# Hybrid streaming encoder step on one core: last SSM group written out with y's split moved ahead of its exponents, bias tables loaded between the slabs

## The reference, cut to what matters

```
h = rmsnorm(x, norm_mix[0])
proj = h @ attn_w_in                       # qi, ki, k, v, q
score = sum_h relu(qi . ki) * wi * IDX_SCALE;  top_k of the visible keys
logits = q . k_sel * ATTN_SCALE + rel_bias[rel_bucket(position difference)]
x = x + softmax(logits) @ v_sel @ attn_w_o;    x = x + mlp(x)
...
z, xBC, dt = rmsnorm(x, norm_mix[1]) @ ssm_w_in;  xBC = silu(conv4(xBC))
# per group g of 8 (4 heads of 64, state 128):
y = (C B^T * decay) (x dt) + C prev_state exp(a_cs) + x * d_skip
y = group_rmsnorm(y * silu(z)) * ssm_norm
x = x + y @ ssm_w_out;    x = x + mlp(x);    out = rmsnorm(x, norm_final)
```

## Time and profile before

| | |
|---|---|
| median of 3 runs | 1992.48 us (1989.91 to 1995.55) |
| the profiled execution | 1994.71 us, its span 1992.7 us |
| mean granted TensorE clock | 0.974 |
| busy: TensorE, VectorE, ScalarE, GpSimd | 1892.0, 1277.9, 796.2, 300.1 us |
| DMA | 176.81 MB, 89 GB/s over the span |

### The profile page before, as it was taken

How to read it: one execution, slowest core, us unless ns; L and a number is a source line. 1 busy time by engine, 2 the same in 40 slices (tenths; PEclk the granted TensorE clock), 3 DMA queues, 4 the chain that set the end, 5 groups by cost and what they waited for, 6 DMA issues and landing times.

```text
span 1992.7 us, 35226 instructions
## 1 busy us (share of the span) xinstructions
PE 1892.0 (95%) x13063; PEld 1769.6 (89%) x13063; DVE 1277.9 (64%) x2367; ACT 796.2 (40%) x1417; POOL 300.1 (15%) x353
## 2 busy tenths in 40 slices
PE   7899888799999999999999999999799999999998
PEld 7777455599999999999889888988699999999998
DVE  4378674435858676546777777777653685858654
ACT  4222473234434343333555345553533443434332
POOL 0001551020000000021333332324102000000001
PEclk9999799999999999998999999999899999999999
DMA  7632102322232223223233443334333222232321
GB/s 163 114 67 51 54 2 92 88 71 79 70 89 77 85 70 102 74 66 90 80 115 124 124 135 89 116 112 127 130 106 105 71 73 80 81 89 69 92 75 53
DMA packets 311565, 176.81 MB, mean 89 GB/s; under 512 B 39888, under 2 KB 305040, under 8 KB 310416
## 3 DMA queue, kind: packets, MB, share of 16 engines
q1 hardware_dynamic: 308752, 172.49, 30.6%
q10 hardware_dynamic: 2688, 2.62, 0.4%
HBM read 155.18 MB, written 19.72 MB: 88 GB/s over the span
## 4 chain that ended last, share of the span: by engine, by line
PE 66%; DVE 5%; ACT 4%; issue 4%; DVEq 0%; ACTq 0%
PE psum L1326 26%; PE psum L204 20%; PE psum L1354 13%; DVE prev L711 2%; PE psum L583 1%; DVE conv_out L700 1%; ACT WH L194 1%; PE psum L587 1%; PE psum L570 1%; PE psum L536 1%; ACT L975 1%; ACT Wm L923 1%; ACT HH L1435 0%; PE psum L611 0%; ACT prevT L883 0%
## 5 line engine op out<-in xcount | busy, mean ns | idle before, releaser
L204 PE MATMUL psum<-b2H,WH 128*128 128x320 f32 x912 | 218.9, 321 | 13.1 <-DVE b2L L1137 12.2
L204 PE MATMUL psum<-b2H,WL 128*128 128x320 f32 x912 | 209.5, 311 | 0.0
L204 PE MATMUL psum<-b2L,WH 128*128 128x320 f32 x912 | 209.4, 311 | 0.0
L194 ACT ACTIVATE WH<-W 128x1024 fp32r<-128x1024 f32 x90 | 95.0, 1056 | 232.8 <-PE psum L204 206.9
L1326 PE MATMUL psum<-b2H,HT 128*128 128x320 f32 x816 | 186.3, 310 | 1.1 <-DVE xT L423 1.1
L1326 PE MATMUL psum<-b2L,HT 128*128 128x320 f32 x816 | 186.0, 309 | 0.0
L204 PEld LDWEIGHTS psum<-b2H,WH 128*128 128x128 f32 x912 | 151.0, 191 | 27.7 <-issue 26.5
L198 DVE TENSOR_TENSOR WL<-W,WH 128x1024 fp32r<-128x1024 f32 x90 | 134.4, 1494 | 55.1 <-ACT WH L194 54.7
L1354 PE MATMUL psum<-HH,HT 128*128 128x320 f32 x544 | 167.4, 308 | 1.5 <-DVE HL L1443 1.5
L1354 PE MATMUL psum<-HL,HT 128*128 128x320 f32 x544 | 167.8, 308 | 0.0
L204 PEld LDWEIGHTS psum<-b2L,WH 128*128 128x128 f32 x912 | 154.3, 190 | 0.0
(11 more groups left out here) (393 smaller groups left out, 4436.1 us busy)
## 6 DMA issues: line engine op xcount, KB each, us to landing
W<-ssm_w_in SPq DMA_DIRECT2D x98, 256.0 KB, 3.1
RW<-mlp_w_up SPq DMA_DIRECT2D x64, 256.0 KB, 3.0
RWx<-mlp_w_up SPq DMA_DIRECT2D x64, 256.0 KB, 3.1
RW<-mlp_w_down SPq DMA_DIRECT2D x64, 256.0 KB, 3.1
RWx<-mlp_w_down SPq DMA_DIRECT2D x64, 256.0 KB, 3.2
bc<-scratch_acs SPq DMA_DIRECT2D x8, 1280.0 KB, 7.6
W<-attn_w_in SPq DMA_DIRECT2D x32, 256.0 KB, 3.7
prev<-state_ssm SPq DMA_DIRECT2D x16, 512.0 KB, 5.2
```

The lines of the kernel that those rows point to most:

```text
L194: act.activation(WH[:, b.slot], W[:, b.slot], ACT.Copy).then_inc(w_hi, 1)
L204: last = pe.matmul(psum[0:m, 2 * b.slot + h, 0:TH], w[:, b.slot, k, 0:m], r[:, k, h * TH:(h + 1) * TH], start=(n == 0 and i == 0), stop=(n ...
```

## The change

Two places. At the start the bias product goes to banks 2 and 3 and the turned vectors to bank 0. TensorE begins slab 0's chunks once the vectors are copied, and slab 1's chunks come one step later in the interleaving and wait for the bias copy. ScalarE makes the high parts of x chunks 2 and 3 ahead of slab 1's split, and VectorE does x's low parts 2 and 3 and the copy of chunk 4 ahead of its part of slab 1's split. SP issues four biasP loads, slab 5, four biasP loads, slab 6, the biasS loads and then slabs 7 and 8.

In the SSM, ScalarE's and VectorE's loops run over groups 2 to 6, and group 7 is written out with `last=True`. There ScalarE makes y's high parts 0 to 7 between the two halves of group 7's exponents. VectorE does the first two states of group 7, the scaling of group 6's y and y's low parts 0 to 3, then its `split_lo` of block B_OUT+1, then low parts 4 to 7 and the last two states. TensorE's, GpSimd's and SP's lists keep their order there.

```diff
     def prompt_states(dve, g):
-        n = 13 * g
+        first_states(dve, g)
+        later_states(dve, g, 1, 4)
+
+    def first_states(dve, g):
         dve.wait_ge(tCS, g + 1)
...
         dve.tensor_copy(ST[:, 0], cs[:, 0:256]).then_inc(sts, 1)
-        for t in range(1, 4):
+
+    def later_states(dve, g, t0, t1):
+        n, cs = 13 * g, bank(4, 1024, 2)
+        for t in range(t0, t1):
...
@@ ssm_group_dve
-        z_evac(dve, g, 1, (lambda: y_scaled(dve, u)) if L else None)
-        prompt_states(dve, g)
+        if last:
+            ssm_last_dve(dve, g, u)
+        else:
+            z_evac(dve, g, 1, (lambda: y_scaled(dve, u)) if L else None)
+            prompt_states(dve, g)
+
+    def ssm_last_dve(dve, g, u):
+        def then():
+            first_states(dve, g)
+            later_states(dve, g, 1, 2)
+            y_scaled(dve, u)
+            for k in range(4):
+                y_split_dve(dve, k)
+        z_evac(dve, g, 1, then)
+        for k in range(4, 8):
+            y_split_dve(dve, k)
+        later_states(dve, g, 2, 4)
@@ ssm_group_act
-        exponents(act, g, lambda: split_hi(act, b0(5), 4))
+        def halfway():
+            split_hi(act, b0(5), 4)
+            if last:
+                for k in range(8):
+                    y_split_act(act, k)
+        exponents(act, g, halfway)
@@ tail_act (tail_dve alike)
-        with act.Fori(2, SG) as g:
+        with act.Fori(2, SG - 1) as g:
             ssm_group_act(act, g, g - 1)
+        ssm_group_act(act, SG - 1, SG - 2, True)
         u = SG - 1
-        for k in range(8):
-            y_split_act(act, k)
@@ SP
-            for p0 in range(0, P, DS):
-                sp.dma_start(biasP[p0:p0 + DS], ...)
+            for p0 in range(0, 64, DS):
+                load_bias_p(p0)
+            load_slab(sp, Block(5), slab_g1(5))
+            for p0 in range(64, P, DS):
+                load_bias_p(p0)
+            load_slab(sp, Block(6), slab_g1(6))
             for gj in range(8):
                 sp.dma_start(biasS[DS * gj:DS * gj + DS], ...)
...
-            for b in range(5, 9):
-                load_slab(sp, Block(b), slab_g1(b))
+            load_slab(sp, Block(7), slab_g1(7))
+            load_slab(sp, Block(8), slab_g1(8))
@@ TensorE
-            pe.matmul(psum[0:NH, 0, 0:512], rb_stage[:], oh_stage[:, 0:512], start=True, stop=True)
-            pe.matmul(psum[0:NH, 1, 0:NREL - 512], ...)
+            pe.matmul(psum[0:NH, 2, 0:512], rb_stage[:], oh_stage[:, 0:512], start=True, stop=True)
+            pe.matmul(psum[0:NH, 3, 0:NREL - 512], ...)
-                pe.transpose(psum[:, 2, col:col + rows], ...).then_inc(v_turn, 1)
-            pe.wait_ge(v_rdy, 5)
+                pe.transpose(psum[:, 0, col:col + rows], ...).then_inc(v_turn, 1)
+            pe.wait_ge(v_rdy, 4)
             first_products(0, 0)
             turn_x(4)
             first_products(0, 1)
-            first_products(1, 0)
             turn_x(5)
             first_products(0, 2)
-            first_products(1, 1)
+            pe.wait_ge(v_rdy, 5)
+            first_products(1, 0)
...
@@ ScalarE
             x_hi(1)
+            x_hi(2)
+            x_hi(3)
             split_hi(act, Block(1))
-            x_hi(2)
             act.wait_ge(v_turn, 2)
+            act.wait_ge(v_rdy, 4)
...
@@ VectorE
-            split_lo(dve, Block(1))
-            chunk_lo(dve, 2, 2, 0, b1H, b1L)
-            for d in range(4, KC):
+            chunk_lo(dve, 2, 2, 0, b1H, b1L)
+            take_x(4)
+            chunk_lo(dve, 3, 3, 0, b1H, b1L)
+            split_lo(dve, Block(1))
+            for d in range(5, KC):
```

More of the change, by code:

```diff
@@ L792, in y_scaled, with ssm_group_dve @@
                                      ALU.mult, ALU.mult).then_inc(yo, 1)
-    def ssm_group_dve(dve, g, u):
+    def ssm_group_dve(dve, g, u, last=False):
         L = u is not None
@@ L929, in exp_w, with ssm_group_act @@
         act.activation(Wm[:], Wm[:], ACT.Exp, scale=-1.0).then_inc(ee, 1)
-    def ssm_group_act(act, g, u):
+    def ssm_group_act(act, g, u, last=False):
         L = u is not None
@@ L2017, in tail_dve @@
         ssm_group_dve(dve, 1, 0)
-        with dve.Fori(2, SG) as g:
+        with dve.Fori(2, SG - 1) as g:
             ssm_group_dve(dve, g, g - 1)
+        ssm_group_dve(dve, SG - 1, SG - 2, True)
         u = SG - 1
-        for k in range(8):
-            y_split_dve(dve, k)
         add_to_x(dve, Block(B_OUT), 0)
@@ L2088, in _, with load_bias_p @@
             bt = S["bias"]
-            for p0 in range(0, P, DS):
+            def load_bias_p(p0):
                 sp.dma_start(biasP[p0:p0 + DS], skew(bt, -REL0 - P - p0, [[NREL - 1, DS], [DS * NREL, NH], [1, 256]])
                              ).then_inc(bias_in, 16)
+            for p0 in range(0, 64, DS):
[4 more added lines that the diff above has]
+            load_slab(sp, Block(6), slab_g1(6))
             for gj in range(8):
@@ L2252, in _ @@
             pe.wait_ge(c_in, 112)
-            pe.matmul(psum[0:NH, 0, 0:512], rb_stage[:], oh_stage[:, 0:512], start=True, stop=True)
-            pe.matmul(psum[0:NH, 1, 0:NREL - 512], rb_stage[:], oh_stage[:, 512:NREL],
+            pe.matmul(psum[0:NH, 2, 0:512], rb_stage[:], oh_stage[:, 0:512], start=True, stop=True)
+            pe.matmul(psum[0:NH, 3, 0:NREL - 512], rb_stage[:], oh_stage[:, 512:NREL],
                       start=True, stop=True).then_inc(v_turn, 1)
             for n, (rows, col) in enumerate(((56, 0), (P, 64), (32, 192))):
-                pe.transpose(psum[:, 2, col:col + rows], v_stage[0:rows, n], ident[0:rows, 0:rows]).then_inc(v_turn, 1)
-            pe.wait_ge(v_rdy, 5)
+                pe.transpose(psum[:, 0, col:col + rows], v_stage[0:rows, n], ident[0:rows, 0:rows]).then_inc(v_turn, 1)
+            pe.wait_ge(v_rdy, 4)
             first_products(0, 0)
@@ L2261, in _ @@
             first_products(0, 1)
-            first_products(1, 0)
             turn_x(5)
             first_products(0, 2)
-            first_products(1, 1)
+            pe.wait_ge(v_rdy, 5)
+            first_products(1, 0)
             turn_x(6)
             first_products(0, 3)
-            first_products(1, 2)
+            first_products(1, 1)
             turn_x(7)
             first_products(0, 4)
+            first_products(1, 2)
             first_products(1, 3)
@@ L2533, in _ @@
             x_hi(1)
+            x_hi(2)
+            x_hi(3)
             split_hi(act, Block(1))
-            x_hi(2)
             act.wait_ge(v_turn, 2)
-            act.activation(tb_stage[:], psum[0:NH, 0:2, :].rearrange("p a b -> p (a b)")[:, 0:NREL], ACT.Copy).then_inc(v_rdy, 1)
+            act.wait_ge(v_rdy, 4)
+            act.activation(tb_stage[:], psum[0:NH, 2:4, :].rearrange("p a b -> p (a b)")[:, 0:NREL], ACT.Copy).then_inc(v_rdy, 1)
             for t in range(NT):
-                if t < 4:
-                    x_hi(t + 3)
+                if t < 3:
+                    x_hi(t + 4)
                 x_squares(t)
@@ L2682, in _ @@
             for dst, n0, w in ((vcol[:, 16:56], 16, 40), (cw[:].rearrange("p t r -> p (t r)"), 64, P), (cb_[:], 192, 32)):
-                dve.tensor_copy(dst, psum[:, 2, n0:n0 + w]).then_inc(v_rdy, 1)
+                dve.tensor_copy(dst, psum[:, 0, n0:n0 + w]).then_inc(v_rdy, 1)
+            chunk_lo(dve, 2, 2, 0, b1H, b1L)
+            take_x(4)
+            chunk_lo(dve, 3, 3, 0, b1H, b1L)
             split_lo(dve, Block(1))
-            chunk_lo(dve, 2, 2, 0, b1H, b1L)
-            for d in range(4, KC):
+            for d in range(5, KC):
                 take_x(d)
```

## The result

The changed kernel takes 1970.87 us (median of four, 1970.02 to 1977.16), the kernel before, run beside it, 1992.18. The ratio is 0.9898 [0.9873, 0.9924], 20.3 us less (25.3 to 15.1). Forecast: 1972, 20.6 us less. Timed a second time beside other experiments, it gave 0.9898 [0.9877, 0.9918] and a median of 1970.67 us. One of those six executions was a slow one of 9095 us; it isn't in the ratio, and the median without it is 1970.20. The profiled execution is the slowest of its four (1977.16 us, span 1975.4, mean granted clock 0.976), so I read it for places and durations, and the profile of the second timing (span 1968.4, clock 0.980) for lengths of stages.

A forecast was written before the change was run, and what follows sets the result against it. TensorE, busy 95% of the span, was taken to bound the kernel through its stands and low clock. Start 8.9 us plus handover 11.7 makes 20.6 off 1992.48: forecast 1972, range 1966 to 1981.

The forecast's parts named there:

- First product: Kernel start: TensorE begins at 15.35, 2.5 us earlier, of which 1.6 us is kept at slab 2's products (bounds 0 and 2.5).
- Bias loads: SP's queue between slabs: the 5.16 us stand ahead of slab 5 goes, and 2.1 us of slow clock with it.
- the covers: Slack between a slab's split and TensorE's demand behind the bias loads: 4.7 us for slab 5, 2.4 for slab 6.
- Rival (b): Bias part yields only 1.6 us: slab 5 not ahead, or slab 6 takes the stand over; 1979 us, chance 0.10.
- two halves of 0.9: Slab 5's load behind four biasP loads: each half takes 0.9 us, an estimate, so it lands at 49.8.
- The later stages have no time of their own: After the start each stage waits on the one before, so the start's 8.9 us gain passes through whole.
- Handover: Last SSM group to output projection: stand 2.8 us for 12.2, gain 11.4 us, less 0.3 for a new wait.
- the new wait of 0.3 for the sample states: Second output block: VectorE's states end at 1424.3, TensorE asks at 1424.1; 0.3 us wait, bounds 0 and 2.
- Written-out group: Last SSM group outside the loop on VectorE and ScalarE: shorter stand there, gain 0.6 us, bounds 0 and 1.0.
- (a): The handover gives 3 to 8 us back, through the clock and waits without cover; 1975 to 1980 us, chance 0.19.
- (c): The handover yields nothing because y's loads are what really ends the wait; 1983.5 us, chance 0.06.
- (d): Slower: engines wait for the new code of the last group written out; 1998 us and up, chance 0.03.

The follow-up runs named there:

- six_ahead: The changed kernel with six biasP loads, not four, ahead of slab 5 on SP; 1973.13 us, ratio 0.9919 to the kernel before.
- eight_ahead: The changed kernel with all eight biasP loads ahead of slabs 5 and 6, biasS still behind; 1973.97 us, ratio 0.9923 to the kernel before.
- start_only: The kernel before with only the start changed (banks, first products, order of loads on SP), SSM as before; 1984.0 us, ratio 0.9972.
- product_held: The kernel before with GpSimd's product of weights in the last group held until y's eight low parts are done; 1988.28 us, ratio 0.9985.
- states_first_both: The changed kernel with both halves of VectorE's sample states ahead of the slab splits in each SSM group; 1943.68 us, ratio 0.9752 to the kernel before.
- written_out_only: The kernel before with ScalarE's and VectorE's group 7 written out behind a shorter loop, nothing moved; 1988.83 us, ratio 0.9984.
- handover_only: The kernel before with only the SSM changed (group 7 written out, y's parts moved), start as before; 1976.69 us, ratio 0.9929.
- states_first_1: The changed kernel with the second half of VectorE's sample states ahead of the second slab split per SSM group; 1943.14 us, ratio 0.9756 to the kernel before.
- states_first_0: The changed kernel with the first half of VectorE's sample states ahead of the first slab split per SSM group; 1946.72 us, ratio 0.9770 to the kernel before.

## Why the prediction was right, step by step

**First product.** Right to a tenth: start 15.30 (15.35 said), slab 2 36.61 (36.55), 1.6 us kept of 2.5. That is nearer than profiles agree: slab 2's product lies at 36.8 to 37.7 in the others with this start, and at 37.8 to 39.9 in those with the old one.

**Bias loads.** The stand went, and with it the low clock after it: 7.5 us from slab 2's product to the 2.18 us stand, 7.3 said; with the first product 9.1, 8.9 said. But the covers were mis-sized. Slab 5's halves landed 10.5 and 12.4 us after issue, at 49.2 and 51.7, where I had both by 49.8. Slab 6's high part began at 62.26 and its split ended at 64.57, where I had 62.5, against a demand near 65.0: 0.45 us of cover in place of 2.4. Rival (b), slab 6 takes the stand over, was half a microsecond away. The step that fails is the price of a slab behind the bias loads, "two halves of 0.9": the second half landed 2.5 us behind the first here and 4.5 in `six_ahead`. Adding up what stands ahead missed slab 5's landing by 1.9 us here, by 2.4 in `six_ahead` (58.2 for 55.8) and by 1.1 the other way in `eight_ahead` (58.9 for 60): it is an estimate, and no bound.

**What the start gave back.** The timed gain of `start_only` is 5.6 us (2.8 to 8.6) where its profile has 8.5 at the 2.18 stand. The interval just reaches that, so the loss is likely and not shown. If it is real, "The later stages have no time of their own" is the step that doesn't hold, and the clock is where the profiles differ. After the 2.18 us stand it fell in six of the seven profiles with four loads ahead of slab 5 (all but `start_only`) and in one of the five with the old order (`product_held`). Such a fall costs 1.6 us: from this stand to the next that all share (2.06 us, released by VectorE's Rs) TensorE takes 82.1 us in the changed kernel, and 80.5 in the kernel before and in `start_only`. The whole attention stage, from the 2.18 us stand to the first product after attention, takes 292.3 us in the profile after, 286.7 at the second timing and 285.7 to 287.4 in the five others with four loads ahead, against 281.8 to 287.3 in the five with the old order. Its length goes with the granted clock: a mean of 0.96 in the profile of 281.8 us, 0.93 in those of 285.8 (before) and 286.7, 0.91 in that of 292.3. That the low clock comes of the change isn't shown: the two ranges overlap.

**Handover.** The gain from the start of the idle time to the read of group 7's state is 36.45 less 25.88, 10.6 us; 11.1 was said for it with the clock up, 9.2 with the clock down. The parts: the stand 2.59 (2.8 said), low parts 0.82 (0.81). The clock fell, which I took not to happen: from its start to the transposes at 1404.89 TensorE takes 4.88 us, against 3.98 in `states_first_both`, where the first pair takes 0.53 and the clock stayed up. So the fall cost 0.9 and not 1.9. The wait of 0.5 for low part 4 shows there, as 0.23 of the 3.98, and not in the changed kernel, where TensorE comes later with its clock down. y's loads landed 5.7 and 8.5 us after issue, faster than I had, so the exponents resumed 2.5 us after TensorE's start in place of 3.4, and the new wait of 0.3 for the sample states didn't come: they end at 1416.89, and TensorE asks at 1418.53. The order of what is late was right: product, shut-out split ending 1.1 after it, states.

**Written-out group.** 0.6 said, bounds 0 and 1.0; measured 3.2 (0.8 to 5.6). In the profile of `written_out_only` the stand ahead of the read gives 0.5, about what I said, and 2.2 come behind it. This term was mis-sized, for its bounds took in the stand and not the clock after it. Why the low clock ended sooner after that read isn't settled; the whole change shows it too (38.37 us from the read to the idle time), and so does `handover_only`.

**Why the sum still met.** In the changed kernel's profile the written-out group gives 1.7 us ahead of the handover (0.4 of stand, 1.3 of clock) for 0.6 said, and the handover 10.6 for 11.1: together 12.3 for 11.7. By the timed halves it is 14.1 (11.4 to 16.7) for 11.7, and 5.6 (2.8 to 8.6) for 8.9. The mechanisms and their places were right; that the two misses lie opposite each other is luck, and the median's nearness to 1972 owes something to it.

**Rivals.** (a) happened in its clock part only, by 0.9 us. (b) nearly: see slab 6. (c) is excluded by `handover_only`, which gains with y's loads left as they were. But the loads have no cover left: the second, issued at 1391.5, landed 8.5 us later, at 1400.0, just when the fifth high part was due, and the eight take 5.34 us for 5.11 before. (d): neither in the changed kernel nor in `written_out_only` does a gap appear where ScalarE or VectorE leaves its loop.

**Open.** Whether the new order of loads brings the low clock of the attention stage. The stage varies by 5.5 us among profiles of the old order alone, with the clock, so twelve profiles don't settle it.

## What to carry to other kernels

When an engine's operation takes several times its usual duration, look at what GpSimd does at that time, and move the reader of PSUM beside it in place of the one with two SBUF inputs; where an order is by hand, ask in every repetition of a loop which work stands behind a wait that it doesn't need, for that was worth 27 us here, more than both parts of the change. A transfer queued behind others need not land when the sum of what stands ahead says: slab 5 missed that sum by up to 2.4 us, more than the 2.1 of one bias load. Leave cover for more than one transfer. Price a stand with the clock after it, and take both levels into the bounds.

## What the runs showed of the hardware

The clock's fall doesn't follow the length of a stand alone. In the changed kernel's profile the read at 1103.87 stood for 3.09 us and the granted clock is 1.00 over 1100 to 1110. The read at 1166.01 stood for 3.09 too and takes 1.07, at full speed, but the clock fell just behind it (1.00 over 1165 to 1167, 0.57 over 1167 to 1171). The read at 1359.05 stood for 2.65 and takes 1.93. The 2.18 us stand brought the clock down at 102.12, and at 113.16 in `product_held`, and not in the kernel before at 111.21. At the handover, after 2.59 or 2.60 us, the first pair takes 0.87 in `handover_only`, `six_ahead`, `eight_ahead`, `states_first_1` and both profiles of the changed kernel. It takes 0.53 in `states_first_0`, where the clock falls 1.3 us later (0.57 over 1373 to 1377), and 0.53 in `states_first_both`, where it stays up. So one operation at full speed behind a stand doesn't show that the clock stayed up; the granted clock of the next few us does.

A VectorE operation with two SBUF inputs that meets GpSimd's product ends 1.08 or 1.09 us after it (1153.80, 1202.31, 1414.82, and the same 1.08 in all seven groups of the profile before), also where it begins half a microsecond ahead of the product's end. That is its own 1.22 less 0.14, so the product let none of its main part run before. Before the change y's first low part, 0.81 by itself, ended about 0.7 after the product, again its own time less 0.1. The Trainium skill ("SBUF — State Buffer", Who interferes with whom) calls the port pair that the two engines share an exclusive lock; by it a VectorE instruction with two SBUF inputs contends with a GpSimd instruction that reads SBUF, and one with at most one SBUF input doesn't. These rows agree, and so do the sample states, with one operand in PSUM: 2.16 us beside the product and 2.15 without it.

Loads of 256 KB held SP at its issuing once enough stood in the queue. In the changed kernel the first four biasP issues took 1.9 us of its time and the last four, behind slab 5, 7.8. In the kernel before all eight took 3.9 and it was the slabs behind them that were held: slab 5's second half took 2.96 us to issue.
